# Norm of the second layer: squares, roots and scaling moved into the first layer's output projection

## The chip, the cores and the metric

The kernel runs on one core of a Trainium2 chip, as one launch. Its time is the device time of that launch in microseconds (us), and the number compared is the median of several runs. One further execution was recorded by the hardware profiler; all rows below are from it. The engines are called PE (matrix products and transposes), DVE (vector), ACT (scalar functions), POOL, and SP, which here only starts transfers.

## What is computed

One inference step of a decoder with two layers, for a prompt of 1024 rows and 8 samples of 4 rows each, with rows of 1024 numbers in fp32. For each layer:

```
h = rmsnorm(x, norm_g) * (1 + scale(c)) + shift(c)
y = mixers(h @ w_in) @ w_out
x = x + gate(c) * y
rmsnorm(x, g) = x * rsqrt(mean(x*x, over the row) + 1e-6) * g
```

The prompt has one condition vector c, each sample has its own. After the second layer a last rmsnorm gives the output. What is changed here is who computes the row factors 1/sqrt(mean + 1e-6) of the second layer's first rmsnorm, and who multiplies x by them, and when.

## The kernel before, in words

The rows are kept as 9 row tiles (RT = 9): 8 tiles of 128 prompt rows and one of 32 sample rows. The program is a sequence of blocks. Inside a block each engine has its own list of instructions, written out by hand, and they meet through semaphores; all engines meet at the end of a block, so nothing of the next block starts before the last engine is done with this one.

Four blocks stand around the change.

**The first layer's output projection** (`output_projection`, layer 0). Its 18 units are (half h of the 1024 output columns, row tile r), in the order (0,0), (0,1), (1,0), (1,1), then (0,r), (1,r) for r = 2 to 8. PE runs 24 matmuls per unit (L2703) into one of 4 banks; DVE multiplies the bank by the gate (L2752) and adds it to x (L2755). After a tile's first unit, DVE also splits the next tile's mixer output into two parts (`split_mix`, L175 and L176), which PE must have before that tile. SP stores each finished tile of x to `x_mid` in HBM (L170), because SBUF does not hold x through the second layer; the end of the block waits until these stores have landed. In the second layer's call of the same function, DVE and ACT do the last rmsnorm tile by tile: ACT squares and sums (L2772), DVE takes the mean (L2724), ACT the root (L2775), DVE the reciprocal (L2726) and the product with x and g (L2727), for tile r-1 after the update of tile r. In the first layer's call this part is skipped.

**The handing back of semaphores** (`give_back_semaphores`, L156), a barrier.

**The second layer's norm** (`normalise`, layer 1). SP starts the loads of the first two blocks of `w_in`. ACT squares all 9 tiles (L587). Then one root (L590) and one reciprocal (L625) for all tiles. DVE scales the 9 tiles into `xn` (L628). PE turns them, four tiles at a time, so that rows stand along the free axis: 8 column slices for tiles 0 to 3, 8 for tiles 4 to 7, 8 small ones for the samples (L614), each into one of 4 banks. DVE (L632) and ACT (L594) take the slices out in turn with scale and shift into `hT`; DVE takes out the sample slices one by one, two instructions each (L639, L641).

**The second layer's input projection** (`project`), whose first unit (L850) needs the whole of the norm's block to be over, and `w_in`.

Of the kernel before, what the change touches and what calls it, by code (L numbers as in the profile page):

```python
# [11 lines left out]
ALU = mybir.AluOpType  # L12
# [546 lines left out]
def normalise(k, layer):  # L559

    nc, t = k.nc, k.t
    groups = [range(0, 4), range(4, 8), range(8, 9)]
    with ExitStack() as st:
        xn = k.sb(st, f"xn{layer}", [P, RT, D])
        ss = k.sb(st, f"ss{layer}", [P, RT])
        sd = k.sb(st, f"sd{layer}", [P, RT])
        cleared = k.sem(st, f"norm_cleared{layer}")
        squared = k.sem(st, f"norm_squared{layer}")
        mean = k.sem(st, f"norm_mean{layer}")
        root = k.sem(st, f"norm_root{layer}")  # L570
        scaled = k.sem(st, f"norm_scaled{layer}")
        turned = k.sem(st, f"norm_turned{layer}")
        read_act = k.sem(st, f"norm_read_act{layer}")
        read_dve = k.sem(st, f"norm_read_dve{layer}")
        with nc.Block() as block:  # L575
            @block.sync
            def _(sp):
                if layer == 1:
                    for j in range(len(k.w1_loaded)):
                        sp.dma_start(k.w1[:, j], t["w_in1"][j].rearrange("p (a n) -> p a n", a=KT)).then_inc(k.w1_loaded[j], 16)  # L580

            @block.scalar
            def _(act):
                act.wait_ge(cleared, 1)
                for r in range(RT):
                    n, _ = row_tile(r)
                    last = act.activation(xn[0:n, r, :], k.x[0:n, r, :], ACT.Square, accum_out=ss[0:n, r:r + 1])  # L587
                last.then_inc(squared, 1)
                act.wait_ge(mean, 1)
                act.activation(sd[:, :], sd[:, :], ACT.Sqrt).then_inc(root, 1)  # L590
                for g in range(2):
                    for a in range(1, KT, 2):
                        act.wait_ge(turned, g * KT + a + 1)
                        act.activation(k.hT[:, a, g * 512:(g + 1) * 512], k.bank[a % 4][:, :], ACT.Identity,  # L594
                                       bias=k.mod_b[:, a, 0:1], scale=k.mod_a[:, a, 0:1]).then_inc(read_act, 1)

            @block.tensor
            def _(pe):
                u = 0
                for g, rows in enumerate(groups):  # L600
                    pe.wait_ge(scaled, rows[-1] + 1)
                    for a in range(KT):
                        if u >= 4:

                            p = u - 4
                            if p >= 2 * KT:
                                pe.wait_ge(read_dve, p - KT + 1)
                            elif p % 2:
                                pe.wait_ge(read_act, p // 2 + 1)
                            else:  # L610
                                pe.wait_ge(read_dve, p // 2 + 1)
                        for j, r in enumerate(rows):
                            n, _ = row_tile(r)
                            last = pe.transpose(k.bank[u % 4][:, j * P:j * P + n], xn[0:n, r, a * P:(a + 1) * P],  # L614
                                                k.const("ident", n)[:, 0:n])
                        last.then_inc(turned, 1)
                        u += 1

            @block.vector
            def _(dve):  # L620
                dve.memset(ss[:, :], 1.0).then_inc(cleared, 1)
                dve.wait_ge(squared, 1)
                dve.tensor_scalar(sd[:, :], ss[:, :], 1.0 / D, EPS, ALU.mult, ALU.add).then_inc(mean, 1)
                dve.wait_ge(root, 1)
                k.dve_order.link(dve, dve.reciprocal(sd[:, :], sd[:, :]))  # L625
                for r in range(RT):
                    n, _ = row_tile(r)
                    dve.tensor_scalar(xn[0:n, r, :], k.x[0:n, r, :], sd[0:n, r:r + 1], None, ALU.mult).then_inc(scaled, 1)  # L628
                for g in range(2):
                    for a in range(0, KT, 2):  # L630
                        dve.wait_ge(turned, g * KT + a + 1)
                        dve.tensor_scalar(k.hT[:, a, g * 512:(g + 1) * 512], k.bank[a % 4][:, :], k.mod_a[:, a, 0:1],  # L632
                                          k.mod_b[:, a, 0:1], ALU.mult, ALU.add).then_inc(read_dve, 1)
                for a in range(KT):
                    dve.wait_ge(turned, 2 * KT + a + 1)
                    o = k.hT[:, a, SEQ:R].rearrange("p (b t) -> p b t", t=DS)
                    sc = k.mod_a[:, a, 1:NC].unsqueeze(2).to_broadcast([P, DB, DS])
                    sh = k.mod_b[:, a, 1:NC].unsqueeze(2).to_broadcast([P, DB, DS])
                    k.dve_order.link(dve, dve.tensor_tensor(  # L639
                        o, k.bank[a % 4][:, 0:NS].rearrange("p (b t) -> p b t", t=DS), sc, ALU.mult))  # L640
                    dve.tensor_tensor(o, o, sh, ALU.add).then_inc(read_dve, 1)  # L641


def project(k, layer):
# [1971 lines left out]
def output_projection(k, layer):  # L2616
# [3 lines left out]
    with ExitStack() as st:  # L2620
# [16 lines left out]
        units = [(0, 0), (0, 1), (1, 0), (1, 1), *((h, r) for r in range(2, RT) for h in range(2))]  # L2637
        units_to = [max(u for u, x in enumerate(units) if x[1] == r) + 1 for r in range(RT)]
        quarter = lambda c: slice(c * KT // 2, (c + 1) * KT // 2)
        if layer == 1:  # L2640
            g = k.sb(st, "final_g", [P, D])
            grow = k.sb(st, "final_g_row", [1, D])
            junk = k.sb(st, "final_junk", [P, D])
            ss = k.sb(st, "final_ss", [P, RT])
            g_loaded = k.sem(st, "final_loaded")
            squared = k.sem(st, "final_squared")
            mean = k.sem(st, "final_mean")
            root = k.sem(st, "final_root")
            done = k.sem(st, "final_done")
        with nc.Block() as block:  # L2650
            @block.sync
            def _(sp):
# [14 lines left out]
                if layer == 0:  # L2667
                    for r in range(RT):
                        n, r0 = row_tile(r)
                        sp.wait_ge(updated, units_to[r])  # L2670
                        k.store(sp, k.x_mid[r0:r0 + n, :], k.x[0:n, r, :])
                else:
                    for r in range(RT):
                        n, r0 = row_tile(r)
                        sp.wait_ge(done, r + 1)
                        k.store(sp, t["y_p"][r0:r0 + n, :] if r < RT - 1 else t["y_s"], k.x[0:n, r, :])
# [30 lines left out]
            def _(dve):  # L2707
# [12 lines left out]
                def scale(r):  # L2720
                    n, _ = row_tile(r)
                    s = ss[0:n, r:r + 1]
                    dve.wait_ge(squared, r + 1)
                    dve.tensor_scalar(s, s, 1.0 / D, EPS, ALU.mult, ALU.add).then_inc(mean, 1)  # L2724
                    dve.wait_ge(root, r + 1)
                    k.dve_order.link(dve, dve.reciprocal(s, s))  # L2726
                    dve.scalar_tensor_tensor(k.x[0:n, r, :], k.x[0:n, r, :], s, g[0:n, :], ALU.mult, ALU.mult).then_inc(done, 1)  # L2727

                split_mix(0)
                split_mix(1)  # L2730
# [13 lines left out]
                for u, (h, r) in enumerate(units):  # L2744
                    n, _ = row_tile(r)
                    if h == 1 and u >= 3 and r < RT - 1:
                        split_mix(r + 1)
                    if u == 0:
                        dve.wait_ge(x_loaded, 32)
                    gates = gate if r < RT - 1 else gate_s  # L2750
                    dve.wait_ge(product, u + 1)
                    dve.tensor_tensor(y[0:n, u % 2, :], k.bank[u % 4][0:n, :], gates[0:n, h * 512:(h + 1) * 512], ALU.mult).then_inc(taken, 1)  # L2752
                    dve.wait_ge(taken, u + 1)
                    xs = k.x[0:n, r, h * 512:(h + 1) * 512]
                    dve.tensor_tensor(xs, xs, y[0:n, u % 2, :], ALU.add).then_inc(updated, 1)  # L2755
                    if layer == 1 and h == 1 and r >= 1:
                        scale(r - 1)
                if layer == 1:
                    scale(RT - 1)

            @block.scalar
            def _(act):
                for h in range(2):
                    for c in range(2):
                        act.wait_ge(loaded[h][c], 16)
                        act.activation(w[:, h, 0, quarter(c)], raw[:, quarter(c), :], ACT.Copy).then_inc(w_rounded, 1)
                if layer == 0:
                    return
                for r in range(RT):
                    n, _ = row_tile(r)  # L2770
                    act.wait_ge(updated, units_to[r])
# [60 lines left out]
```

## Time and profile before

| | us |
|---|---|
| median of 3 runs | 2133.75 (2133.3 to 2138.24) |
| the profiled execution's own time | 2137.92 |
| its span, first to last instruction | 2136.1 |
| PE busy | 1816.2 (85%) |
| DVE busy | 1115.4 (52%) |
| ACT busy | 678.9 (32%) |
| mean granted clock of PE, share of full | 0.912 |

Engines work side by side, so the busy times do not add up to the span. The profiled execution took 4.17 us longer than the median of the runs, and 0.32 us less than the slowest of them.

### The profile page before, as it was taken

The page shows a single profiled execution, that of the slowest core. Times are in us where ns is not written, and L with a number is a line of the kernel's source. Part 1 is how long each engine was busy: PE and PEld are TensorE (multiplying, and loading weights), DVE is VectorE, ACT ScalarE, POOL GpSimd, SP SyncE. Part 2 cuts the span into 40 slices and gives each one's busy share as a digit, 9 for nine tenths or more (in the row PEclk, how much of TensorE's full clock was granted, in tenths as well). Part 3 has the DMA queues.
Part 4 walks back from the last instruction along what each step waited for, and adds up shares of the span by engine and source line. Part 5 has one row for each costly group of instructions (what it writes and reads, how often), then busy time and mean ns, then how long its engine had stood idle before and what let it go on. Part 6 is the DMA issues. An engine that isn't in the chain of part 4 may idle for free. (4 is left out here: it accounts for less than half of the span.)

```text
span 2136.1 us, 29341 instructions
## 1 busy us (share of the span) xinstructions
PE 1816.2 (85%) x11673; PEld 1283.7 (60%) x11685; DVE 1115.4 (52%) x2314; ACT 678.9 (32%) x1689; POOL 215.8 (10%) x202
## 2 busy tenths in 40 slices
PE   3699997768999967679699999999986899788698
PEld 2699997235665634458476676665554466444386
DVE  2421003646777764244302699981894799233354
ACT  3411120636665501210212210102663466232211
POOL 1232120000000071100000100000002000322000
PEclk9799998658999988779899999999997899999699
DMA  7321111520000084541101111110002000796131
GB/s 248 147 70 52 45 58 46 195 83 1 1 2 1 2 332 200 197 160 60 63 26 41 64 39 41 41 41 1 1 1 73 7 1 2 294 373 267 62 140 52
DMA packets 36165, 188.54 MB, mean 88 GB/s; under 512 B 5916, under 2 KB 6013, under 8 KB 19452
## 3 DMA queue, kind: packets, MB, share of 16 engines
q0 software_dynamic: 17296, 102.82, 12.3%
q1 hardware_dynamic: 18734, 83.84, 10.7%
q8 instruction: 94, 1.54, 0.3%
q14 instruction: 41, 0.34, 0.1%
HBM read 171.69 MB, written 19.12 MB: 89 GB/s over the span
## 5 line engine op out<-in xcount | busy, mean ns | idle before, releaser
L853 PE MATMUL banks<-hT,w_in 128*128 128x352 f32 x864 | 256.5, 459 | 0.0
L853 PEld LDWEIGHTS banks<-hT,w_in 128*128 128x128 f32 x864 | 163.9, 190 | 90.7
L2703 PE MATMUL banks<-w_out_parts,mix_parts 128*128 128x512 f32 (+1 forms) x864 | 203.3, 398 | 12.1 <-DVE w_out_parts L2717 8.8
L2703 PEld LDWEIGHTS banks<-w_out_parts,mix_parts 128*128 128x128 f32 (+1 forms) x864 | 158.5, 184 | 58.3 <-issue 11.2
L1417 ACT ACTIVATE nsa_p<-banks,nsa_negmax 128x512 f32<-128x512 f32 (+3 forms) x192 | 104.1, 554 | 94.8 <-DVE nsa_negmax L1334 94.7
L848 PE MATMUL banks<-hT_rest,w_in_high 128*128 128x352 f32 x384 | 124.5, 324 | 0.0
L848 PE MATMUL banks<-hT_high,w_in_rest 128*128 128x352 f32 x384 | 124.4, 324 | 0.0
L848 PE MATMUL banks<-hT_high,w_in_high 128*128 128x352 f32 x384 | 124.2, 324 | 0.0
L1334 DVE TENSOR_REDUCE nsa_negmax<-banks 128x2 f32<-128x1024 f32 (+4 forms) x77 | 84.7, 1100 | 70.2 <-PE banks L1286 58.4
L850 PE MATMUL banks<-w_in,hT 128*128 128x256 f32 (+3 forms) x576 | 119.1, 361 | 1.3 <-PEq L575 1.3
L850 PEld LDWEIGHTS banks<-w_in,hT 128*128 128x128 f32 (+1 forms) x576 | 93.9, 185 | 24.3 <-issue 10.7
L1860 DVE TENSOR_SCALAR_CACHE_REDUCE dsa_mask<-mix,prompt_top_bits 128x384 bf16<-128x384 f32 (+2 forms) x102 | 89.8, 943 | 0.6
L1301 PE MATMUL banks<-cf,nsa_p 128*128 128x128 f32 x544 | 76.1, 280 | 15.9 <-ACT nsa_pT L1258 13.1
L959 ACT ACTIVATE mix<-banks 128x352 f32<-128x352 f32 x48 | 22.2, 464 | 191.6 <-PE banks L853 91.2
L1301 PEld LDWEIGHTS banks<-cf,nsa_p 128*128 128x128 f32 x544 | 59.2, 143 | 36.5 <-issue 20.8
L2026 PE MATMUL banks<-cf,l_ring 128*128 128x128 f32 x384 | 62.9, 305 | 20.5 <-DMA l_ring<-in_diff_k_cache,rows 8.4
L1860 DVE TENSOR_SCALAR_CACHE_REDUCE dsa_mask<-prompt_top_upper,prompt_top_bits 128x384 bf16<-128x384 bf16 (+2 forms) x90 | 79.2, 943 | 0.5
L843 PE MATMUL banks<-w_in_high,hT_high 128*128 128x264 f32 (+1 forms) x216 | 64.6, 299 | 16.1 <-DVE hT_rest L875 16.1
L894 DVE TENSOR_SCALAR qT<-banks 128x352 f32<-128x352 f32 x12 | 6.3, 525 | 133.1 <-PE banks L848 133.1
L1334 DVE TENSOR_REDUCE diff_negmax<-banks 128x2 f32<-128x1024 f32 (+3 forms) x38 | 44.3, 1166 | 59.8 <-PE banks L1286 58.3
L848 PEld LDWEIGHTS banks<-hT_high,w_in_high 128*128 128x128 f32 x384 | 72.3, 188 | 0.0
L848 PEld LDWEIGHTS banks<-hT_high,w_in_rest 128*128 128x128 f32 x384 | 72.2, 188 | 0.0
(562 smaller groups left out, 3505.0 us busy)
## 6 DMA issues: line engine op xcount, KB each, us to landing
w_in<-in_w_in SPq DMA_DIRECT2D x24, 1056.0 KB, 4.9
ada_w<-in_ada SPq DMA_DIRECT2D x24, 1024.0 KB, 4.9
w_out<-in_l_w_out SPq DMA_DIRECT2D x8, 1024.0 KB, 5.4
x_in<-in_x_prompt SPq DMA_DIRECT2D x2, 2048.0 KB, 24.6
nsa_ring<-in_state_l_win_kv POOLq DMA_DIRECT2D x8, 512.0 KB, 6.2
x_after<-in_x_prompt SPq DMA_DIRECT2D x1, 4096.0 KB, 15.5
x_mid<-x_after SPq DMA_DIRECT2D x8, 512.0 KB
x_after<-x_mid SPq DMA_DIRECT2D x1, 4096.0 KB, 15.6
```

The source lines that it names most:

```text
L843: last = pe.matmul(bank[0:rows, 0:n], lhs, rhs, start=a == 0 and x == 0, stop=a == KT - 1 and x == 2)
L848: last = pe.matmul(bank[:, 0:cn], lhs, rhs, start=a == 0 and x == 0, stop=a == KT - 1 and x == 2)
L850: last = pe.matmul(bank[0:rows, 0:n], k.hT[:, a, r0:r0 + rows], w[:, j % slots, a, 0:n], start=(a == 0), stop=(a == KT - 1))
L853: last = pe.matmul(bank[:, 0:cn], w[:, j % slots, a, m * P:(m + 1) * P], k.hT[:, a, c0:c0 + cn], start=(a == 0), stop=(a == KT - 1))
L894: last = dve.tensor_scalar(k.qT[:, what + m, c0:c0 + cn], bank[:, 0:cn], SCALE, None, ALU.mult)
L959: act.activation(k.mix[:, what + m, c0:c0 + cn], k.bank[i % 4][:, 0:cn], ACT.Silu).then_inc(free[i % 4], 1)
L1301: last = pe.transpose(k.bank[4 + c % 2][:, i * P:(i + 1) * P], p_sb[:, u % SLOTS, col:col + P], k.const("ident"))
L1334: last = dve.tensor_reduce(of_unit(nm, u), scores_of(u), X, ALU.max, negate=True)
L1417: last = act.activation(slot_of(u)[:, g, x], scores_of(u)[:, g, x], ACT.Exp, bias=of_unit(nm, u)[:, g, x:x + 1], accum_out=of_unit(rs, u)[ ...
L1860: last = dve.tensor_scalar(m, v, threshold(j), None, op, ALU.add, accum_out=seen[:, j:j + 1])
L2026: last = pe.transpose(o[:, j * P:(j + 1) * P], ring.run[:, g % ring.slots, c % 2 * 4 + j, k_col[m]:k_col[m] + P], k.const("ident"))
L2703: last = pe.matmul(k.bank[u % 4][0:n, :], lhs, rhs, start=a == 0 and x == 0, stop=a == KT - 1 and x == 2)
```

## The change

The first layer's output projection gets the same four steps per tile that the second one has: square and sum, mean, root, reciprocal, and then a product of x with the row factor, in place and without g. Before DVE overwrites a tile with its scaled form, it waits until the store of the unscaled tile to `x_mid` has landed. SP waits for each store before it goes on to the next. The norm's block loses all of this and keeps the loads of `w_in`, the turns, and the scale and shift. It now uses 8 banks, and all 8 sample slices go into one bank, from which DVE takes them with two instructions. The diff, cut to its core:

```diff
 def normalise(k, layer):
-        xn = k.sb(st, f"xn{layer}", [P, RT, D])
-        ...
             def _(act):
-                act.wait_ge(cleared, 1)
-                for r in range(RT):
-                    n, _ = row_tile(r)
-                    last = act.activation(xn[0:n, r, :], k.x[0:n, r, :], ACT.Square, accum_out=ss[0:n, r:r + 1])
-                last.then_inc(squared, 1)
-                act.wait_ge(mean, 1)
-                act.activation(sd[:, :], sd[:, :], ACT.Sqrt).then_inc(root, 1)
                 for g in range(2):
                     for a in range(1, KT, 2):
                         act.wait_ge(turned, g * KT + a + 1)
...
             def _(pe):
                 for g, rows in enumerate(groups):
-                    pe.wait_ge(scaled, rows[-1] + 1)
                     for a in range(KT):
-                        if u >= 4:
-                            ...
+                        if g == 1 and a % 2:
+                            pe.wait_ge(read_act, a // 2 + 1)
+                        elif g == 1:
+                            pe.wait_ge(read_dve, a // 2 + 1)
+                        elif g == 2 and a == 0:
+                            pe.wait_ge(read_dve, KT // 2 + 1)
                         for j, r in enumerate(rows):
                             n, _ = row_tile(r)
+                            o = k.bank[a][:, j * P:j * P + n] if g < 2 else k.bank[0][:, a * NS:(a + 1) * NS]
+                            last = pe.transpose(o, k.x[0:n, r, a * P:(a + 1) * P], k.const("ident", n)[:, 0:n])
+                        if g < 2 or a == KT - 1:
+                            last.then_inc(turned, 1)
...
             def _(dve):
-                dve.memset(ss[:, :], 1.0).then_inc(cleared, 1)
-                dve.wait_ge(squared, 1)
-                dve.tensor_scalar(sd[:, :], ss[:, :], 1.0 / D, EPS, ALU.mult, ALU.add).then_inc(mean, 1)
-                dve.wait_ge(root, 1)
-                k.dve_order.link(dve, dve.reciprocal(sd[:, :], sd[:, :]))
-                for r in range(RT):
-                    n, _ = row_tile(r)
-                    dve.tensor_scalar(xn[0:n, r, :], k.x[0:n, r, :], sd[0:n, r:r + 1], None, ALU.mult).then_inc(scaled, 1)
...
-                for a in range(KT):
-                    dve.wait_ge(turned, 2 * KT + a + 1)
-                    ... (two tensor_tensor for each of the 8 slices)
+                dve.wait_ge(turned, 2 * KT + 1)
+                o = k.hT[:, :, SEQ:R].rearrange("p a (b t) -> p a b t", t=DS)
+                sc, sh = (x[:, :, 1:NC].unsqueeze(3).to_broadcast([P, KT, DB, DS]) for x in (k.mod_a, k.mod_b))
+                k.dve_order.link(dve, dve.tensor_tensor(o, k.bank[0][:, 0:KT * NS].rearrange("p (a b t) -> p a b t", a=KT, t=DS), sc, ALU.mult))
+                dve.tensor_tensor(o, o, sh, ALU.add)

 def output_projection(k, layer):
                         sp.wait_ge(updated, units_to[r])
-                        k.store(sp, k.x_mid[r0:r0 + n, :], k.x[0:n, r, :])
+                        sp.dma_start(k.x_mid[r0:r0 + n, :], k.x[0:n, r, :]).then_inc(mid_stored, 16)
+                        sp.wait_ge(mid_stored, 16 * (r + 1))
...
                     k.dve_order.link(dve, dve.reciprocal(s, s))
-                    dve.scalar_tensor_tensor(k.x[0:n, r, :], k.x[0:n, r, :], s, g[0:n, :], ALU.mult, ALU.mult).then_inc(done, 1)
+                    x = k.x[0:n, r, :]
+                    if layer == 0:
+                        dve.wait_ge(mid_stored, 16 * (r + 1))
+                        dve.tensor_scalar(x, x, s, None, ALU.mult).then_inc(done, 1)
+                    else:
+                        dve.scalar_tensor_tensor(x, x, s, g[0:n, :], ALU.mult, ALU.mult).then_inc(done, 1)
...
-                    if layer == 1 and h == 1 and r >= 1:
+                    if h == 1 and r >= 1:
                         scale(r - 1)
-                if layer == 1:
-                    scale(RT - 1)
+                scale(RT - 1)
...
-                if layer == 0:
-                    return
                 for r in range(RT):
                     n, _ = row_tile(r)
                     act.wait_ge(updated, units_to[r])
```

## Rows read from the trace of the kernel before

**Rows 1.** Windows: length, busy time (count) of PE, PEld, DVE, ACT, POOL; PEclk, DMA, GB/s.

```profile
1020.00:1041.00 21.00, 20.85 (x91) 12.93 (x90) 5.17 (x10) 0.00 (x0) 0.00 (x0) 1.00 0.12 50
...
1052.50:1059.70 7.20, 0.00 (x0) 0.00 (x0) 3.14 (x7) 4.14 (x8) 0.00 (x0) 0.50 0.00 0
```

**Rows 2.** Timeline, norm block: start, length, what, [idle before <-releaser].

```profile
1045.51 0.82 SPq L580 DMA_DIRECT2D w_in<-in_w_in  x2
1045.59 0.07 DVE L621 MEMSET ss<- 128x9 f32 x1 [3.31 <-PEq L156]
...
1055.16 1.28 ACT L590 ACT_TABLE_LOAD   x1
...
1059.75 3.42 PE L614 MATMUL banks<-cf,xn 128*128 128x128 f32 x16 [18.90 <-DVE xn L628]
...
1072.06 0.19 DVE L641 TENSOR_TENSOR hT<-hT,mod_b 128x32 f32<-128x32 f32 x1
...
1072.57 5.50 PE L850 MATMUL banks<-w_in,hT 128*128 128x132 f32 x32 [1.33 <-PEq L575]
...
1078.02 1.97 PE L850 MATMUL banks<-w_in,hT 128*128 128x132 f32 x16
```

**Rows 3.** Single lines of the source: duration ns min/median/max, first and last start.

```profile
L628 DVE TENSOR_SCALAR xn<-x_after,sd x9: 734/749/753, 1057.0 to 1062.3; 128x1024 f32<-128x1024 f32 x8, 32x1024 f32<-32x1024 f32 x1
...
L632 DVE TENSOR_SCALAR hT<-banks,mod_a,mod_b x8: 790/810/814, 1062.9 to 1068.8; 128x512 f32<-128x512 f32 x8
```

**Rows 4.** Timeline, the first layer's norm: the same turns.

```profile
43.62 6.33 PE L466 MATMUL banks<-cf,x_in 128*128 128x128 f32 x32
...
52.96 3.71 PE L466 MATMUL banks<-cf,x_in 128*128 128x128 f32 x32
...
59.69 0.68 PE L473 MATMUL banks<-cf,x_in 32*128 32x32 f32 x8
...
71.47 0.42 DVE L519 TENSOR_TENSOR hT<-hT,mod_a 128x256 f32<-128x256 f32 x1 [9.78 <-ACT mod_a L383]
```

**Rows 5.** Windows of PE alone: length, busy (count), granted clock, DMA, GB/s.

```profile
1045.50:1046.00 0.50, 0.00 (x0) 0.70 0.00 0
1059.70:1062.50 2.80, 2.75 (x13) 0.50 0.02 6
...
1063.00:1069.00 6.00, 5.40 (x50) 1.00 0.00 0
1069.30:1072.50 3.20, 1.39 (x8) 1.00 0.00 0
...
1073.00:1076.00 3.00, 3.00 (x16) 0.50 0.00 0
```

**Rows 6.** Timeline of PE: its one gap in each output projection.

```profile
962.54 2.74 PE L2703 MATMUL banks<-w_out_parts,mix_parts 128*128 128x512 f32 x8 [2.35 <-DVE mix_parts L176]
2052.06 8.23 PE L2703 MATMUL banks<-w_out_parts,mix_parts 128*128 128x512 f32 x35 [0.98 <-DVE mix_parts L176]
```

**Rows 7.** Timeline of DVE in the first output projection, tiles 2 and 3.

```profile
969.93 0.69 DVE L2752 TENSOR_TENSOR y<-banks,gate_rows 128x512 f32<-128x512 f32 x1 [6.12 <-PE banks L2703]
...
980.81 0.69 DVE L2752 TENSOR_TENSOR y<-banks,gate_rows 128x512 f32<-128x512 f32 x1 [4.02 <-PE banks L2703]
```

**Rows 8.** Timeline, end of the second output projection.

```profile
2129.50 0.68 DVE L2755 TENSOR_TENSOR x_after<-x_after,y 32x512 f32<-32x512 f32 x1
...
2130.11 0.13 DVE L2724 TENSOR_SCALAR final_ss<-final_ss 128x1 f32<-128x1 f32 x1
...
2130.71 1.29 DVE L2727 SCALAR_TENSOR_TENSOR x_after<-x_after,final_ss,final_g 128x1024 f32<-128x1024 f32 x1
...
2131.33 0.18 ACT L2772 ACTIVATION_READ_ACCUMULATOR final_junk<-x_after 32x1 f32 x1
```

**Rows 9.** Timeline of DVE, last update of the first output projection.

```profile
1041.60 0.68 DVE L2755 TENSOR_TENSOR x_after<-x_after,y 32x512 f32<-32x512 f32 x1
```

**Rows 10.** Source line of both output projections' block end, SP: first and last start.

```profile
L2650 SPq COMPARE_BRANCH  x2: 33/33/33, 1044.3 to 2135.8; - x2
```

More of the change, by code:

```diff
@@ L563, in normalise @@
     with ExitStack() as st:
-        xn = k.sb(st, f"xn{layer}", [P, RT, D])
[L565 to L571, printed above, removed]
         turned = k.sem(st, f"norm_turned{layer}")
@@ L577, in _ @@
             def _(sp):
-                if layer == 1:
-                    for j in range(len(k.w1_loaded)):
-                        sp.dma_start(k.w1[:, j], t["w_in1"][j].rearrange("p (a n) -> p a n", a=KT)).then_inc(k.w1_loaded[j], 16)
+                for j in range(len(k.w1_loaded)):
+                    sp.dma_start(k.w1[:, j], t["w_in1"][j].rearrange("p (a n) -> p a n", a=KT)).then_inc(k.w1_loaded[j], 16)
             @block.scalar
             def _(act):
-                act.wait_ge(cleared, 1)
-                for r in range(RT):
-                    n, _ = row_tile(r)
-                    last = act.activation(xn[0:n, r, :], k.x[0:n, r, :], ACT.Square, accum_out=ss[0:n, r:r + 1])
-                last.then_inc(squared, 1)
-                act.wait_ge(mean, 1)
-                act.activation(sd[:, :], sd[:, :], ACT.Sqrt).then_inc(root, 1)
                 for g in range(2):
@@ L593, in _ @@
                         act.wait_ge(turned, g * KT + a + 1)
-                        act.activation(k.hT[:, a, g * 512:(g + 1) * 512], k.bank[a % 4][:, :], ACT.Identity,
+                        act.activation(k.hT[:, a, g * 512:(g + 1) * 512], k.bank[a][:, :], ACT.Identity,
                                        bias=k.mod_b[:, a, 0:1], scale=k.mod_a[:, a, 0:1]).then_inc(read_act, 1)
@@ L598, in _ @@
             def _(pe):
-                u = 0
                 for g, rows in enumerate(groups):
-                    pe.wait_ge(scaled, rows[-1] + 1)
                     for a in range(KT):
-                        if u >= 4:
[L605 to L611, printed above, removed]
+                        if g == 1 and a % 2:
[4 more added lines that the diff above has]
+                            pe.wait_ge(read_dve, KT // 2 + 1)
                         for j, r in enumerate(rows):
                             n, _ = row_tile(r)
[L614 to L617, printed above, removed]
+                            o = k.bank[a][:, j * P:j * P + n] if g < 2 else k.bank[0][:, a * NS:(a + 1) * NS]
+                            last = pe.transpose(o, k.x[0:n, r, a * P:(a + 1) * P], k.const("ident", n)[:, 0:n])
+                        if g < 2 or a == KT - 1:
+                            last.then_inc(turned, 1)
             @block.vector
             def _(dve):
-                dve.memset(ss[:, :], 1.0).then_inc(cleared, 1)
-                dve.wait_ge(squared, 1)
-                dve.tensor_scalar(sd[:, :], ss[:, :], 1.0 / D, EPS, ALU.mult, ALU.add).then_inc(mean, 1)
-                dve.wait_ge(root, 1)
-                k.dve_order.link(dve, dve.reciprocal(sd[:, :], sd[:, :]))
-                for r in range(RT):
-                    n, _ = row_tile(r)
-                    dve.tensor_scalar(xn[0:n, r, :], k.x[0:n, r, :], sd[0:n, r:r + 1], None, ALU.mult).then_inc(scaled, 1)
                 for g in range(2):
@@ L631, in _ @@
                         dve.wait_ge(turned, g * KT + a + 1)
-                        dve.tensor_scalar(k.hT[:, a, g * 512:(g + 1) * 512], k.bank[a % 4][:, :], k.mod_a[:, a, 0:1],
+                        dve.tensor_scalar(k.hT[:, a, g * 512:(g + 1) * 512], k.bank[a][:, :], k.mod_a[:, a, 0:1],
                                           k.mod_b[:, a, 0:1], ALU.mult, ALU.add).then_inc(read_dve, 1)
-                for a in range(KT):
-                    dve.wait_ge(turned, 2 * KT + a + 1)
[L636 to L641, printed above, removed]
+                dve.wait_ge(turned, 2 * KT + 1)
[3 more added lines that the diff above has]
+                dve.tensor_tensor(o, o, sh, ALU.add)
 def project(k, layer):
@@ L2642, in output_projection @@
             grow = k.sb(st, "final_g_row", [1, D])
-            junk = k.sb(st, "final_junk", [P, D])
-            ss = k.sb(st, "final_ss", [P, RT])
             g_loaded = k.sem(st, "final_loaded")
[L2646 to L2649, printed above, removed]
+        else:
+            mid_stored = k.sem(st, "x_mid_stored")
+        junk = k.sb(st, f"out_junk{layer}", [P, D])
+        ss = k.sb(st, f"out_ss{layer}", [P, RT])
+        squared = k.sem(st, f"out_squared{layer}")
+        mean = k.sem(st, f"out_mean{layer}")
+        root = k.sem(st, f"out_root{layer}")
+        done = k.sem(st, f"out_done{layer}")
         with nc.Block() as block:
@@ L2726, in scale @@
                     k.dve_order.link(dve, dve.reciprocal(s, s))
-                    dve.scalar_tensor_tensor(k.x[0:n, r, :], k.x[0:n, r, :], s, g[0:n, :], ALU.mult, ALU.mult).then_inc(done, 1)
+                    x = k.x[0:n, r, :]
+                    if layer == 0:
+                        dve.wait_ge(mid_stored, 16 * (r + 1))
+                        dve.tensor_scalar(x, x, s, None, ALU.mult).then_inc(done, 1)
+                    else:
+                        dve.scalar_tensor_tensor(x, x, s, g[0:n, :], ALU.mult, ALU.mult).then_inc(done, 1)
                 split_mix(0)
@@ L2755, in _ @@
                     dve.tensor_tensor(xs, xs, y[0:n, u % 2, :], ALU.add).then_inc(updated, 1)
-                    if layer == 1 and h == 1 and r >= 1:
+                    if h == 1 and r >= 1:
                         scale(r - 1)
-                if layer == 1:
-                    scale(RT - 1)
+                scale(RT - 1)
             @block.scalar
```

## The prediction

> **What bounds the kernel now.** I read the windows by stage first, to find which engine has no pause around the change. In the first output projection PE is busy 20.85 of 21.00 us, while DVE has half its time free and ACT all of it [rows 1]: PE sets the pace there, and what DVE and ACT do between two banks costs nothing until PE waits for it. Then I read the timeline of the norm's block [rows 2]. Its engines start at 1045.5, PE's first turn comes at 1059.75 after it sat idle for 18.9 us, and the first matmul of the next block comes at 1072.57. Here the engines take turns: ACT squares nine tiles, loads a table, DVE scales the first four tiles, and only then does PE start. From the barrier to the next block's first matmul it is 1072.57 - 1045.51 = 27.06 us, and all of it lies on the path, because the blocks are divided by barriers and the only transfer that crosses this one, `w_in`, is over by 1052.5: the DMA share after it is 0.00 [rows 1]. After the block PE is dense again at once [rows 2]. So each microsecond taken out of the 27.06 moves everything behind it forward by one, unless the next block comes to wait for `w_in`.
>
> **The change, part by part.** Removed from the norm's block: squares, table load, root, reciprocal, and the wait for the scaled tiles. What stays is a chain with PE at its head, and I build its length anew from the block's start.
>
> Start: DVE's first instruction came 0.08 after SP's [rows 2]; PE's I take at 0.1.
>
> Turns of the prompt: 64 transposes. Their price has two ends. The first layer's norm turned 32 in 3.71 us [rows 4], 0.116 each; the first 16 of this block took 3.42 [rows 2], 0.214 each. The windows of PE say which holds when: the first 2.80 us ran at a granted clock of 0.50, and from 1063.00 on it was 1.00 [rows 5]; these are the levels 1.2 and 2.4 GHz. PE had stopped at 1040.85 [rows 1], and the clock fell inside 1045.5 to 1046.0 [rows 5]. After the change PE restarts near 1046.35, just behind that fall, so I take a start at the low level, and for its length the 3.0 us of this block. The far row is the first layer's 32 turns in 6.33 [rows 4], which is the slow price for some 5.5 us. At full pace 64 cost 7.42; each slow microsecond loses 1 - 0.116/0.214 = 0.46. That is 7.42 + 1.4 = 8.8 us, and 9.9 with the far row. With no slow stretch it would be 7.4.
>
> Does PE wait for the readers? With 8 banks, slices 0 to 7 find free banks. At full pace a bank comes every 0.46, so each reader gets one every 0.93, and DVE needs 0.81 [rows 3]. PE stays the slower one. Before, with 4 banks, it waited only briefly too, so the banks by themselves are worth next to nothing here.
>
> The Trainium skill, "TensorE: Matmul & The Clock Gate", Part 4 (PE-mode transpose), says that transposes do not count as activity for the clock, so that the full clock "doesn't engage" for them. The trace speaks against it: from 1059.75 PE ran nothing but transposes, and after 1063.00 the clock was 1.00 [rows 5]. By the page all 64 would cost 0.214, 13.7 us in place of 8.8; the sum goes by the rows.
>
> Samples: 8 small turns in 0.68 [rows 4]; I take 0.8 with the pause before them. Then one wait and two DVE instructions of 128x256, 0.42 each [rows 4], with 0.1 between: 0.94. Before, this tail was 16 short instructions, one slice after another. From DVE's last end, 1072.25, to the first matmul it was 0.32 [rows 2].
>
> New block: 0.1 + 8.8 + 0.8 + 0.94 + 0.32 = 11.0 us. Removed: 27.06 - 11.0 = 16.1.
>
> Added to the first output projection, per tile: on ACT a square and sum and a root, on DVE mean, reciprocal and a product of 0.75 us (the same form as L628) [rows 3]. The second output projection shows the rhythm: mean at 2130.11, product at 2130.71 [rows 8], so DVE is held 0.60 + 0.75 = 1.35 us per tile. What hides it: a bank comes every (980.81 - 969.93)/2 = 5.44 us, and DVE had waited 4.02 us before the one at 980.81 [rows 7]. What is next in DVE's queue is the gate product of the next bank, and then `split_mix`, about 1.9 us long, which PE needs a whole tile (10.88) after the bank that precedes the scaling. So DVE may be held 10.88 - 1.4 - 1.4 - 1.9 = 6.2 us before PE stands; 1.35 is far from it. The one table load, 1.28 [rows 2], falls on ACT after the first tile's square; DVE's wait for the first root and the first store lies in its 6.12 us of idle before 969.93 [rows 7]. Cost: 0.
>
> The new wait for the store: at the scaling of tile r-1 its store was issued a tile earlier, 10.88 us. The last store was issued at 1042.28 at the earliest and SP was released at 1044.3 [rows 9, 10], 2.0 us for a 32-row tile. Both `w_in` transfers, four times as large in sum as a full tile of 512 KB, were over 7.0 us after the first issue [rows 1, 2]. So a full tile's takes between 2.0 and 7.0, and the wait is 0. SP's own wait holds back only the next store, which isn't due before.
>
> At the end the cover is gone: there is no further matmul. Scaling tiles 7 and 8 lies open, partly behind the last store. By the rhythm of the second output projection, counted from the start of the last update (1041.60) [rows 8, 9]: the product of tile 7 starts 1.21 later, at 1042.81, ends 1043.56; the sum of tile 8's squares is read out 2.01 later, 1043.6; mean to product 0.60, 1044.25; the store has landed at 1044.3; the product ends 1045.05. Before, SP at 1044.3 was the last one. The barrier comes 0.75 us later. Bounds: 0.3 if the instructions overlap more than there, 1.4 if the store lands late.
>
> Saved so far: 16.1 - 0.75 = 15.3 us.
>
> **The clock behind the block.** The next block's first 32 matmuls took 5.50, while 16 later took 1.97 [rows 2], so they lost 5.50 - 3.94 = 1.6 us; the clock was 0.50 from 1073 to 1076 [rows 5]. Before this fall PE had been busy 1.39 of 3.20 us [rows 5], the small turns one by one and the barrier. After the change dense turns go on until a gap of 0.94 + 0.32 = 1.3 us. Two gaps after dense work are on record: 2.35 us in the first output projection, 0.98 in the second [rows 6]; after the first the clock fell (24 matmuls to the bank at 969.93 took 7.4 against 5.44), after the second it did not (35 matmuls in 8.23, 0.235 each). 1.3 is nearer to 0.98, so I take it that this fall goes: 1.6 more. The bounds are 0 and 1.6.
>
> **Sum.** 15.3 + 1.6 = 16.9 us. Against the profiled execution's own 2137.92 that is 2121.0. The median of the runs is 4.17 lower; the removed block holds no part that differs between executions except the clock, so I take the same saving there: 2133.75 - 16.9 = 2116.9, told as 2117.
>
> **Rivals.** (a) *The saving is right, but the clock still falls* behind the block: 15.3, so 2118.5. For it: the gap of 1.3 is above 0.98. (b) *The turns stay slow*, all 64 at 0.214, by the page's rule or because PE's activity isn't dense enough: 13.7 for 8.8, and the fall behind it too: 15.3 - 4.9 = 10.4, so 2123.3. Against it stand the windows [rows 5]; for it, the first layer's slow stretch of twice the length. (c) *`w_in` becomes the bound.* The load starts 0.75 later and is over by 1053.3, the new block at 1057.3; it binds when it takes 4 us longer. Even twice its 7.0 us would end at 1060.3 and cost 3: 2120. (d) *On the other side: the scaling holds PE.* If DVE is held more than 6.2 us per tile, `split_mix` is late, for 6 tiles (3 to 8). Only the wait for the store could do it, and it would have to take 10.88 - 0.6 + 4.9 = 15.2 us from issue to landing before the first microsecond is lost; to eat the 16.9 it takes 18.0 us, and to be slower by 0.3% (6.4 us), 19.1. The rows say at most 7.0. (e) *The work was hidden anyway*, because the next stage waits for something else: no row shows PE waiting for anything but this barrier, and the time would be 2133.
>
> **How the numbers follow.** Forecast 0.55, 2117, by itself 2114.5 to 2119; (a) 0.25; (b) 0.10; (c) 0.04; (d) 0.02; (e) 0.02; and 0.02 for something faster than all of these. The runs before lie 4.9 us apart, so a median may fall some 3 to either side of its sum. The range reaches to (b) above, 2123.5, and below to 2112.5: no slow stretch at all (1.4), a tail of 0.3, and 2.5 of that spread. 0.3% is 6.4 us, about what a measurement of this kernel can tell from no change. Faster by more: 0.95; within: 0.03; slower: 0.02.
>
> **What the profile after would show.** PE's first turn within 0.3 us of the start of the norm's block; the block 11 us long to the next matmul, with 8.8 in the turns; the first output projection with the same pace of banks, 5.44 us, and no wait of PE for `mix_parts` beyond the one there; no DVE wait for `x_mid` except in the last tile; the barrier 0.75 later; a clock of 1.00 in the next block's first 4 us. Wrong would be: turns at 0.21 throughout, a low clock behind them, or a PE wait for DVE within the projection.

## The result, and the profile after

The changed kernel took 2118.66 us, median of 5 runs (2116.81 to 2124.02), against 2133.75 (5 runs, 2133.03 to 2138.24): ratio 0.9924, 95% interval 0.9903 to 0.9945. That is 15.1 us less, with an interval of 12 to 21. The forecast was 2117, with a range of 2112.5 to 2123.5. A later series gave 2119.34 against 2136.38, ratio 0.9916 (0.9889 to 0.9943).

The profiled execution of the changed kernel had a span of 2115.0, 21.1 below that of before. Not all of it is the change: tile 0's first update started 3.0 us earlier already (954.31 against 957.27), and up to there both kernels run the same instructions. So the reading goes by the stretch from the start of the last update to the next block's first matmul. It is 1072.57 - 1041.60 = 30.97 us before [rows 2, 9].

The timeline of the changed kernel over this stretch (start, length, what, idle before and releaser), with lines of DVE, ACT, SP and PE:

```profile
1038.62 0.68 DVE L2732 TENSOR_TENSOR x_after<-x_after,y 32x512 f32<-32x512 f32 x1
...
1039.83 0.75 DVE L2702 TENSOR_SCALAR x_after<-x_after,out_ss 128x1024 f32<-128x1024 f32 x1
1040.45 0.18 ACT L2746 ACTIVATION_READ_ACCUMULATOR out_junk<-x_after 32x1 f32 x1
...
1041.40 0.74 DVE L2702 TENSOR_SCALAR x_after<-x_after,out_ss 32x1024 f32<-32x1024 f32 x1
1043.32 0.83 SPq L571 DMA_DIRECT2D w_in<-in_w_in  x2
...
1043.36 9.25 PE L594 MATMUL banks<-cf,x_after 128*128 128x128 f32 x72 [5.49 <-PEq L156]
...
1052.64 0.42 DVE L608 TENSOR_TENSOR hT<-banks,mod_a 128x256 f32<-128x256 f32 x1 [0.23 <-PE banks L594]
1053.10 0.42 DVE L609 TENSOR_TENSOR hT<-hT,mod_b 128x256 f32<-128x256 f32 x1
...
1053.83 3.84 PE L818 MATMUL banks<-w_in,hT 128*128 128x132 f32 x32 [1.22 <-PEq L567]
```

The whole stretch is 1053.83 - 1038.62 = 15.21 us. All 72 turns run in one piece of 9.25 us; the engines no longer take turns in the block. The last product of x (1041.40) ends at 1042.14, 3.52 us after the start of the last update, where 3.45 was worked out. The first 32 matmuls behind the block take 3.84 us, 5.50 before [rows 2].

The windows of PE alone, same kernel (length, busy and count, granted clock, DMA share, GB/s):

```profile
1042.50:1043.00 0.50, 0.00 (x0) 0.96 0.00 0
1043.00:1043.50 0.50, 0.14 (x1) 0.50 0.00 0
...
1046.00:1046.50 0.50, 0.50 (x5) 0.63 1.10 439
1046.50:1047.00 0.50, 0.50 (x7) 1.00 0.88 372
...
1053.00:1053.50 0.50, 0.00 (x0) 1.00 0.00 0
...
1054.00:1054.50 0.50, 0.50 (x6) 1.00 0.00 0
```

PE starts its turns at a granted clock of 0.50. It has 1.00 from about 1046.4, 3.0 us later, and keeps it through the gap behind the turns.

The cover in the projection, the changed kernel's DVE at the banks that answer to [rows 7]:

```profile
966.95 0.69 DVE L2729 TENSOR_TENSOR y<-banks,gate_rows 128x512 f32<-128x512 f32 x1 [4.82 <-PE banks L2675]
...
977.83 0.69 DVE L2729 TENSOR_TENSOR y<-banks,gate_rows 128x512 f32<-128x512 f32 x1 [2.74 <-PE banks L2675]
```

The distance is 10.88 us, to the hundredth what it was. DVE's idle time before the second bank fell from 4.02 to 2.74, by the 1.3 us of the scaling. DVE waited for none of the stores: a full tile's landed 2.6 us after its issue (median of 8), where the prediction had bounds of 2.0 and 7.0.

### The profile page after: what moved, and what is told of

Its sections match the earlier page's. It is cut to its first block and busy times, and to the rows that moved or that the text cites. A ratio compares the mean times of both kernels' runs of the same rounds, so it can differ in the third digit from the quotient of the medians.

```text
span 2115.0 us, 29387 instructions
## 1 busy us (share of the span) xinstructions
PE 1811.8 (86%) x11685; PEld 1278.2 (60%) x11685; DVE 1116.3 (53%) x2315; ACT 681.2 (32%) x1697; POOL 217.0 (10%) x202
## 5 line engine op out<-in xcount | busy, mean ns | idle before, releaser
L1269 PE MATMUL banks<-cf,nsa_p 128*128 128x128 f32 x544 | 76.1, 280 | 15.9 <-ACT nsa_pT L1226 13.1
L1994 PE MATMUL banks<-cf,l_ring 128*128 128x128 f32 x384 | 64.1, 309 | 20.4 <-DMA l_ring<-in_diff_k_cache,rows 8.7
L1994 PEld LDWEIGHTS banks<-cf,l_ring 128*128 128x128 f32 x384 | 46.9, 156 | 43.2 <-issue 13.8
```

Of the source, the lines that this page charges most:

```text
L1269: last = pe.transpose(k.bank[4 + c % 2][:, i * P:(i + 1) * P], p_sb[:, u % SLOTS, col:col + P], k.const("ident"))
L1994: last = pe.transpose(o[:, j * P:(j + 1) * P], ring.run[:, g % ring.slots, c % 2 * 4 + j, k_col[m]:k_col[m] + P], k.const("ident"))
```

## The experiments

Times scatter by several us from one execution to the next: the kernel before took between 2126.4 and 2146.2 us. So each kernel was profiled and read by the stretch defined above. The fourth column is the length of the first 32 matmuls behind the block, 3.84 at full clock. Each ratio is taken against runs of the kernel before in the same series (medians 2133.75, 2135.1, 2136.59 and 2136.38), so medians of different series compare less well than the ratios do.

| kernel | stretch | of it from w_in issue | first 32 matmuls | median (runs) | ratio, 95% |
|---|---|---|---|---|---|
| before | 30.97 | 27.06 | 5.50 | 2133.75 (5) | |
| changed | 15.21 | 10.51 | 3.84 | 2118.66 (5) | 0.9924 (0.9903 to 0.9945) |
| the move alone | 16.56 | 11.86 | 5.51 | 2123.7 (12) | 0.9952 (0.9935 to 0.9968) |
| the turns alone | 28.57 | 24.65 | 3.84 | 2132.04 (12) | 0.9986 (0.9969 to 1.0003) |
| DVE held 4 us | 16.66 | 11.95 | 3.84 | 2120.72 (7) | 0.993 (0.9907 to 0.9954) |
| DVE held 8 us | 16.63 | 11.93 | 3.84 | 2138.82 (10) | 1.0028 (1.0006 to 1.005) |
| PE kept busy | 13.75 | 9.05 | 3.84 | 2120.29 (8) | 0.9938 (0.9912 to 0.9965) |
| gap behind the block | 16.75 | 12.04 | 5.50 | 2122.83 (10) | 0.9953 (0.9932 to 0.9974) |
| tail cut | 14.71 | 10.71 | 3.84 | 2119.06 (7) | 0.9926 (0.9903 to 0.995) |
| kept busy and tail cut | 13.57 | 9.04 | 3.84 | 2120.31 (8) | 0.9935 (0.991 to 0.996) |
| changed, again | 16.65 | 11.94 | 3.84 | 2119.34 (6) | 0.9916 (0.9889 to 0.9943) |
| kept busy and tail cut, again | 13.57 | 9.04 | 3.84 | 2118.64 (6) | 0.9915 (0.9889 to 0.9941) |

**The move alone.** Against the changed kernel:

```diff
-                        if g == 1 and a % 2: ...
+                        if u >= 4: ... (wait for the bank read four turns ago)
-                            o = k.bank[a][:, j * P:j * P + n] if g < 2 else k.bank[0][:, a * NS:(a + 1) * NS]
+                            o = k.bank[u % 4][:, j * P:j * P + n]
...
+                for a in range(KT):  (two tensor_tensor for each of the 8 sample slices)
```

> Squares, roots and scaling in the first output projection as in the changed kernel, but the norm's block turns as before: 4 banks, the 8 sample slices one by one. My theory: nearly all of the saving is the move. The block from the first w_in issue to the next block's first matmul is then 12.9 to 13.1 us (12.8 from first turn to first matmul as before, plus the start) where the changed kernel has 10.5 and the kernel before 27.06: 14 us less than before. The sparse sample slices stay, so the clock of PE still falls behind the block (first 32 matmuls 5.5 us and not 3.84). Time: 2.4 + 1.6 = 4 us above the changed kernel, ratio to before about 0.9935 to 0.9945. Rival (the saving is in the turns, 8 banks and one sample bank, and the move gives little): the block stays above 20 us and the time is within 5 us of before.

It got 16.56 us, 14.4 less than before. The block was even shorter than expected, 11.9 and not 13: before, DVE was still scaling tiles 4 to 8 when PE filled the first banks and could not read them at once, and PE stood 0.60 us for DVE after its first 16 turns. That is read from the two timelines and was not tested apart. The median is 11.4 us below before (7 to 14), where the stretch says 14.4, and the ratio of 0.9952 lies just above the expected 0.9935 to 0.9945. Its timeline of PE shows what 4 banks and single slices do to the end:

```profile
1043.89 8.74 PE L597 MATMUL banks<-cf,x_after 128*128 128x128 f32 x66 [5.49 <-PEq L156]
1052.86 0.24 PE L597 MATMUL banks<-cf,x_after 32*128 32x32 f32 x1 [0.23 <-DVE hT L607]
1053.26 1.14 PE L597 MATMUL banks<-cf,x_after 32*128 32x32 f32 x5 [0.16 <-ACT hT L578]
```

and its windows of PE show the clock fall, as before [rows 5]:

```profile
1056.00:1056.50 0.50, 0.50 (x7) 1.00 0.00 0
1056.50:1057.00 0.50, 0.50 (x7) 0.85 0.00 0
1057.00:1060.00 3.00, 3.00 (x15) 0.50 0.00 0
```

**The turns alone.** The kernel before, with the changed kernel's banks and sample tail, the turns reading `xn` behind `pe.wait_ge(scaled, rows[-1] + 1)`.

> The other half alone: squares, roots, scaling in the norm's block as before, but turns over 8 banks, and all sample slices in one bank taken out with two instructions. My theory: the 14.2 us before the first turn stay, the turns and the sample tail take 10.4 in place of 12.8, so the block is 24.6 to 24.8 us, and the clock does not fall behind it: 2.4 + 1.6 = 4 us below before, ratio 0.998. Rival (the fall of the clock behind the block has nothing to do with the sparse sample slices and comes by chance): the first 32 matmuls of the next block take 5.5 us here too, and only 2.4 are saved.

It took 28.57 us with no fall behind: 2.4 + 1.66 = 4.1 us less than before in this execution, as expected. The move alone saved 14.4 us and left the fall as it was, so the two halves save 14.4 + 4.06 = 18.5 in sum; together they saved 15.76 + 1.66 = 17.4. The difference of 1.0 lies in the turns, which each half shortens by itself: from the first turn to the next block's first matmul it takes 12.82 us before, 11.83 with the move, 10.42 with the new turns, and 10.47 with both. The time of this kernel, 0.9986 (0.9969 to 1.0003), does not tell it from no change by itself.

**DVE held.** In the first output projection, ahead of the scaling of tiles 0 to 5, with 6 and with 12 instructions:

```diff
+                        if r < 6 and layer == 0:
+                            for _ in range(6):
+                                k.dve_order.link(dve, dve.tensor_tensor(idle[:, :], idle[:, :], idle[:, :], ALU.mult))
```

> The changed kernel with 6 idle DVE instructions (about 0.7 us each, 4.2 us in sum) ahead of the scaling of tiles 0 to 5 in the first output projection: DVE is held about 5.6 us per tile in place of 1.35. My bound for PE's cover was 6.2 us. Expected: PE's pace of 24 matmuls in 5.44 us unchanged, time within 1 us of the changed kernel. Rival (the cover is only the 4.02 us that DVE waits for the next bank): each of 6 tiles costs 1.6 us, 9 to 10 us in sum.

> The same with 12 idle instructions, about 8.5 us: DVE is held about 9.9 us per tile, 3.7 above the bound of 6.2. Expected: split_mix comes late for five or six tiles, PE shows gaps of 3.7 us each before tiles 3 to 8, 18 to 22 us in sum, and the time is near that of the kernel before or above it; if PE's clock falls in these gaps, up to 1.6 us more per tile. Rival (nothing on DVE is on the path here at all): no change. Rival (cover of 4.02): 6 times 5.9, 35 us.

With 4 us more, first to last update takes 84.32 us, and 84.31 in the changed kernel. PE has no pause beyond the one at tile 2 that all have, so the cover is not the 4.02 us that DVE waits. The median is 2.1 us above that of the changed kernel, where 1 was expected. Its profile has 1.45 us more in the stretch, by the longer slow start of the turns told below; beyond that the runs do not tell it from scatter. With 8 us more, the timeline of PE has a pause before each of tiles 3 to 8 (the last column is the idle time and its releaser):

```profile
979.47 11.17 PE L2676 MATMUL banks<-w_out_parts,mix_parts 128*128 128x512 f32 x48 [1.72 <-DVE mix_parts L176]
993.98 13.96 PE L2676 MATMUL banks<-w_out_parts,mix_parts 128*128 128x512 f32 x48 [3.34 <-DVE mix_parts L176]
1008.50 11.18 PE L2676 MATMUL banks<-w_out_parts,mix_parts 128*128 128x512 f32 x48 [0.56 <-DVE mix_parts L176]
1023.01 12.79 PE L2676 MATMUL banks<-w_out_parts,mix_parts 128*128 128x512 f32 x48 [3.34 <-DVE mix_parts L176]
```

A tile takes 993.98 - 979.47 = 14.51 us in place of 10.88, 3.63 more, where 3.7 was expected. DVE's round sets it: PE stands for a part of the round (0.56 to 3.34 us), and for another part it runs below full clock, so that 48 matmuls take 11.17 to 13.96 us. DVE is held for 10.1 us per tile there (966.14 to 976.22), so the cover comes out at 10.1 - 3.6 = 6.5 us. From PE's restart at tile 2 to the start of the last update it is 1064.44 - 964.95 = 99.5 us against 1038.62 - 959.57 = 79.1 in the changed kernel, 20.4 more. The median is 18.1 above that of the kernel held 4 us, in the same series, and 20.2 above the changed kernel's. So a held DVE does stop PE, as rival (d) says, and the limit lies near the 6.2 us of the prediction; the change, with 1.35, stays 5 us away from it.

**PE kept busy.** After the last unit of the first output projection:

```diff
+                if layer == 0:
+                    for _ in range(18):
+                        pe.matmul(k.bank[4][:, :], mix[:, 1, 0, 0, :], w[:, 0, 0, 0, :], start=True, stop=True)
```

> The changed kernel with 18 extra matmuls of 128x512 (0.227 us each, 4.1 us) by PE into a bank that nobody reads, at the end of the first output projection, where PE would be idle until the norm's block. PE's idle time before its first turn falls from 5.5 us to about 1.4. My theory of the clock term: the turns then start at a granted clock of 1.00, the 16 first ones take 1.86 us in place of 3.4, and the block is 1.4 us shorter, 9.1 us; the barrier is not later, since DVE still ends last. Rival (transposes do not hold the full clock): it starts at 1.00 but falls during the 7.4 us of turns. Rival (the slow first turns come from something other than the clock, such as the w_in transfer beside them): the first 16 take 3.4 us all the same.

```profile
1037.95 4.28 PE L2679 MATMUL banks<-w_out_parts,mix_parts 128*128 128x512 f32 x18
...
1043.60 7.79 PE L594 MATMUL banks<-cf,x_after 128*128 128x128 f32 x72 [1.37 <-PEq L156]
```

This timeline has all 72 turns in 7.79 us in place of 9.25, and its windows of PE read a clock of 1.00 all the way:

```profile
1042.00:1043.60 1.60, 0.23 (x3) 1.00 0.00 0
1043.60:1046.00 2.40, 2.40 (x22) 1.00 0.62 137
1046.00:1049.00 3.00, 3.00 (x30) 1.00 1.01 425
```

The clock term is shown, 9.25 - 7.79 = 1.46 us against 1.4, and the `w_in` transfer beside the turns (425 GB/s) is not what made them slow. The median, 2120.29, does not show the gain.

**Gap behind the block.** Two idle copies after DVE's last instruction.

```diff
+                for _ in range(2):
+                    k.dve_order.link(dve, dve.tensor_copy(wait_here[:, :], k.x[:, 0, :]))
```

> The changed kernel with two idle DVE copies of 128x1024 at the end of the norm's block, so that PE's gap between the last small turn and the next block's first matmul grows from 1.2 us to 2.6 to 3.3 (each copy 0.7 to 1.0). My theory: a gap of the length of that in the first output projection (2.35) brings the clock down behind it: the first 32 matmuls take some 5.4 us in place of 3.84. Cost 1.4 to 2 for the copies plus 1.6 for the clock. Rival (the fall came from the sparse turns, not from a gap of this size): only the copies are paid.

```profile
1057.52 5.50 PE L821 MATMUL banks<-w_in,hT 128*128 128x132 f32 x32 [2.88 <-PEq L568]
```

In the timeline PE's gap is 2.88 us, and the next 32 matmuls take 5.50. The turns ahead of it were dense. So there are two ways to this fall, a long gap and sparse turns; the changed kernel avoids both, with a gap of 1.22. That the sparse turns count, and not the 0.1 us by which their gap is longer (1.32 with the move alone, 1.33 before), is shown by the kernel kept busy: its gap of 1.37 us behind dense matmuls left the clock at 1.00.

**Tail cut.** Tile 7 is scaled after unit (0,8), and tile 8's factor is kept for the norm's block:

```diff
+                    if layer == 0 and r == RT - 1:
+                        dve.reciprocal(k.factor8[:, :], s)
+                        return
...
+                dve.tensor_scalar(k.x[0:NS, RT - 1, :], k.x[0:NS, RT - 1, :], k.factor8[:, 0:1], None, ALU.mult).then_inc(scaled, 1)
```

> The changed kernel with less in the open tail: tile 7 is scaled after the sample tile's first unit, and tile 8's product with its factor moves into the norm's block, where DVE is idle before the first bank. My theory: the barrier then comes when SP sees the last store landed, as before the change: from the start of the last update to the w_in issue 3.9 to 4.1 us in place of 4.70, 0.7 us saved, nothing given back. Rival: the sum of squares of tile 8 and its mean still end last, and less than 0.3 us is saved.

From the last update to the `w_in` issue it takes 14.71 - 10.71 = 4.0 us in place of 4.70: 0.7 saved, as expected. But the whole stretch is only 0.5 shorter, where nothing was to be given back: the turns took 9.45 us and not 9.25. PE began them 4.79 us after its last matmul, still at 1.00; the clock fell 0.2 us later, so the whole slow stretch, 1044.70 to 1048.05, lay on the turns, where in the changed kernel the first 0.4 us of it lay ahead of them. At the end of the block SP waits for the store to land, as before the change, and 0.2 us for PE's queue (waiter, releaser, us, times, longest):

```profile
SPq L2625 <- DMA x_mid<-x_after: 1.6, 1, 1.6
SPq L2625 <- PEq L2625: 0.2, 1, 0.2
```

**Both, and both kernels again.**

> The last two together: PE kept busy to the end of the first output projection, and the tail cut. Expected: 0.7 + 1.4 = 2.1 us below the changed kernel in the stretch from the last update to the next block's first matmul (15.2 to 13.1 us); in the time, ratio to before 0.991 against 0.992 for the changed kernel, which the spread of the runs hardly shows. Rival: with the barrier earlier, the extra matmuls end after it is due and give 0.3 us back.

> The changed kernel itself, to see which of its numbers repeat. My theory: the stretch from the start of the last update to the next block's first matmul repeats within 0.3 us of 15.21 unless the slow stretch of the clock is longer than 3 us (up to 16.7, as with the held kernels); what lies outside it differs by several us from one execution to the next with identical instructions. Time 15 to 18 us below before. Rival (the saving is in part chance of the first five runs): less than 12 us below before.

> The version with PE kept busy and the shorter open tail once more, beside the changed kernel on the same chip. My theory: 13.5 to 13.8 us in the stretch, 1.6 to 3 us less than the changed kernel beside it, and the median lower by about as much, 0.1%, within what the runs scatter. Rival (the extra matmuls cost something later, for instance a later fall of the clock): the median is above that of the changed kernel by more than 1 us in both of its series.

The version with both takes 13.57 us in each of its profiles. The forecast for it was 13.1, and the miss is the rival named there: the 18 extra matmuls now end too late. They end 3.37 us after the start of the last update (1051.17 - 1047.80), and the `w_in` issue comes 4.53 us after it, where it was 4.00 with the tail cut alone. SP waits 0.7 us for PE at the end of the block in place of 0.2. So the cut tail gives 0.2 us here and not 0.7; fewer extra matmuls were not tried.

The changed kernel took 16.65 the second time. Its turns:

```profile
1049.30 10.69 PE L594 MATMUL banks<-cf,x_after 128*128 128x128 f32 x72 [5.49 <-PEq L156]
```

They took 10.69 us in place of 9.25; both kernels with DVE held have the same 10.7, with a clock of 0.50 for about 6 us. So the slow stretch at the start of the turns is either 3 or about 6 us long in identical code, and keeping PE busy removes either, 1.5 or 2.9 us. The medians do not resolve this: 2120.31 and 2118.64 against 2118.66 and 2119.34. The version is better in the stretch that it changes, and not shown to be faster as a whole.

## Why the prediction was right

- **What bounds.** That every microsecond of the block lies on the path held: 27.06 became 10.51, and nothing behind it took the time back. `w_in` was not waited for, so rival (c) did not occur.
- **The new block**, 11.0 forecast, 10.51 measured. Turns of the prompt and samples 9.25 (8.8 + 0.8), tail and barrier 1.22 (0.94 + 0.32), start 0.04 (0.1). The turns came out 0.35 shorter because the 8 sample turns were priced too high: at full clock all 72 took 7.79, 0.37 more than the 7.42 worked out for the 64 others, where 0.8 was put. In the three later profiles with the long slow stretch the block was 11.9 us long. Both bounds of that term thus occurred.
- **The open tail**, 0.75 forecast: 4.70 - 3.91 = 0.79.
- **The projection**, 0 forecast: 84.31 us from first to last update, and 84.33 before (957.27 to 1041.60). The bound of 6.2 us held in the test with held DVE, where it came out at about 6.5.
- **The clock behind the block**, 1.6 forecast by the nearer of two gaps: 1.66. Rival (a) was seen in no run with dense turns and a gap of 1.22 us. What made the fall before was not the gap alone but the one-by-one sample slices; with these, the move alone kept it.
- **The sum.** 15.76 + 1.66 = 17.4 us in the profiles, 16.9 forecast; with the long slow stretch it is 16.0. The medians say 15.1 (12 to 21), and 17.0 in the later series. Which execution is profiled decides a part of what two spans differ by: here 3.0 us of the 21.1 lay ahead of the change.
- **The page's rule against this change** was that transposes do not bring up the clock (the Trainium skill, "TensorE: Matmul & The Clock Gate", Part 4). PE ran nothing but turns from 1043.36, and its clock was 1.00 from 1046.5 on; kept busy before, it stayed at 1.00 through 7.8 us of turns. The rule does not hold here. That all 64 turns stay slow, rival (b), was seen in no run.

What was weak was the length given to the slow stretch. One row said 3.0 us and another 5.5, and the sum took the nearer one as if it were fixed. Of the seven profiles in which the moved-up turns met the low clock, three had about 6 us. That the changed kernel's first profile had the short one is chance: the forecast of 16.9 is 0.5 below what that profile shows, and it would have been 0.9 above with the long one.

## What to carry to other kernels

Where engines take turns between two barriers, move the steps that need no barrier into the dense stage ahead, where the idle engines have cover, and work out the cover in the queue of the busy engine's supplier: by the prediction it was 6.2 us per tile here, by the test about 6.5, and both are more than the 4.02 of idle time that the timeline shows. Compare profiles by a stretch between two marks and not by their spans; the two spans of the version with both edits, 2128.9 and 2109.9, differ by more than the whole change gave, while its stretch took 13.57 us in both.

## What the runs showed of the hardware

- After 5.5 us without work PE began its moved-up turns at a clock of 0.50 in all six profiles with such a pause; after 4.79 us, in the tail cut, the clock fell 0.2 us into the turns. It then stayed at 0.50 for 2.7 to 3.4 us of the turns in four of these seven profiles and for about 6 in three. The changed kernel itself shows both lengths.
- A pause of 1.22 us behind dense turns left the clock at 1.00 in all profiles that have one (1.23 in one of them), and so did pauses of 1.19 and 1.37 us behind the extra dense matmuls; 2.88 us brought it down. Behind sparse turns 1.32 us was enough.
- The start of the first projection's last update lay at 1036.39 and at 1047.80 us in the two profiles of one and the same kernel, the version with both edits. PE's granted clock from 810 to 926 us, ahead of that, was 0.76 in the first and 0.70 in the second. What moves it was not tested.
